# Paged key gathers of a decoding step: four issues at once, or one after each of four key transposes

## The reference, cut to what matters

```python
past_c = cache_ckv[l][page_table].reshape(n_s, past, KV_LORA)     # 8 x 4096 x 256
past_r = cache_krope[l][page_table].reshape(n_s, past, ROPE_DIM)  # 8 x 4096 x 32
...
q_lat = jnp.einsum('bthd,chd->bthc', q_nope, w_uk)
s = (jnp.einsum('bthc,blc->bhtl', q_lat, keys_c)
     + jnp.einsum('bthr,blr->bhtl', q_rope, keys_r)).astype(jnp.float32) * ATTN_SCALE
...
pr = jax.nn.softmax(s, axis=-1).astype(keys_c.dtype)
o_lat = jnp.einsum('bhtl,blc->bthc', pr, keys_c)
```

## Time and profile before

| | |
|---|---|
| median of 3 runs | 1775.27 us (1772.91 to 1775.78) |
| the profiled execution, its own time | 1764.69 us |
| its span, first to last instruction | 1762.9 us |
| TensorE busy in the span | 1696.1 us, 96% |
| VectorE, ScalarE, POOL busy | 536.5, 357.0, 163.1 us |
| mean granted TensorE clock | 0.98 of full speed |

### The profile page before, as it was taken

The page is one execution under the profiler, slowest core; times in us unless marked ns, Lnnn a source line. Parts: engine busy times, 40 slices in busy tenths (PEclk is TensorE's granted clock), DMA queues, the critical chain, the costliest instruction groups (busy, mean ns, idle before and its releaser), DMA issues.

```text
span 1762.9 us, 21779 instructions
## 1 busy us (share of the span) xinstructions
PE 1696.1 (96%) x9101; PEld 977.2 (55%) x9102; DVE 536.5 (30%) x1080; ACT 357.0 (20%) x690; POOL 163.1 (9%) x169
## 2 busy tenths in 40 slices
PE   7999999999999999999999999999999999999890
PEld 5556666666666666666666555554444444444340
DVE  1434242423422323232312454541112122221125
ACT  1122323223231121222121111101111111111115
POOL 1000000000001431111000000001111111111110
PEclk9999999999999999999999999989999999999995
DMA  7101111020114454332253442297999999999985
GB/s 209 50 24 40 49 36 49 25 79 30 61 49 138 162 187 172 132 132 108 70 198 108 155 158 84 94 376 279 390 369 387 383 396 385 388 388 392 382 298 201
DMA packets 103347, 335.47 MB, mean 190 GB/s; under 512 B 24346, under 2 KB 68450, under 8 KB 86868
## 3 DMA queue, kind: packets, MB, share of 16 engines
q1 hardware_dynamic: 88516, 274.11, 41.2%
q0 software_dynamic: 13568, 55.78, 9.9%
q10 hardware_dynamic: 1168, 4.23, 0.6%
HBM read 306.84 MB, written 34.45 MB: 194 GB/s over the span
## 4 chain that ended last, share of the span: by engine, by line
PE 90%; DMA 5%; DVE 2%; issue 1%; ACT 1%; POOL 0%; SPq 0%; DVEq 0%; POOLq 0%; ACTq 0%
PE psum L952 13%; PE psum L1062 9%; PE psum L1331 8%; PE psum L1336 7%; PE psum L1214 6%; PE psum L1228 5%; PE psum L1363 4%; PE psum L1357 4%; PE psum L989 4%; PE psum L877 3%; PE psum L1099 3%; PE psum L962 2%; DMA arena<-in_w_up 2%; PE psum L1007 2%; PE psum L1344 2%; PE psum L996 2%
## 5 line engine op out<-in xcount | busy, mean ns | idle before, releaser
L952 PE MATMUL psum<-arena 128*128 128x344 f32 x768 | 244.9, 456 | 0.0
L1062 PE MATMUL psum<-arena 128*128 128x344 f32 x576 | 182.3, 458 | 0.0
L952 PEld LDWEIGHTS psum<-arena 128*128 128x128 f32 x768 | 137.9, 190 | 63.8 <-issue 8.5
L1336 PE MATMUL psum<-arena 128*64 128x512 f32 x320 | 141.6, 595 | 0.7 <-ACT arena L1644 0.7
L1337 PE MATMUL psum<-arena 128*64 128x512 f32 x320 | 141.6, 595 | 0.0
L1331 PE MATMUL psum<-arena 128*128 128x512 f32 x320 | 139.8, 595 | 0.2 <-DVE arena L2213 0.2
L1062 PEld LDWEIGHTS psum<-arena 128*128 128x128 f32 x576 | 103.2, 190 | 53.0 <-issue 11.2
L1214 PE MATMUL psum<-arena 128*128 128x344 f32 x384 | 113.9, 460 | 1.1 <-ACT arena L1614 1.1
L1331 PEld LDWEIGHTS psum<-arena 128*128 128x128 f32 x320 | 60.0, 190 | 72.6 <-issue 72.1
L1228 PE MATMUL psum<-arena 128*128 128x512 f32 x224 | 99.2, 595 | 0.0
L1214 PEld LDWEIGHTS psum<-arena 128*128 128x128 f32 x384 | 74.3, 194 | 40.7 <-issue 3.7
(11 more groups left out here) (358 smaller groups left out, 2061.9 us busy)
## 6 DMA issues: line engine op xcount, KB each, us to landing
arena<-in_w_gate SPq DMA_DIRECT2D x32, 2048.0 KB, 20.3
arena<-in_w_up SPq DMA_DIRECT2D x32, 2048.0 KB, 25.9
arena<-in_w_down SPq DMA_DIRECT2D x32, 2048.0 KB, 32.1
arena<-in_w_in SPq DMA_DIRECT2D x33, 512.0 KB, 4.2
gates<-arena SPq DMA_DIRECT2D x16, 516.0 KB, 5.0
arena<-gates SPq DMA_DIRECT2D x16, 516.0 KB, 4.9
arena<-in_x_prompt SPq DMA_DIRECT2D x16, 512.0 KB, 4.2
arena<-in_w_o SPq DMA_DIRECT2D x1, 4096.0 KB, 18.3
```

Of the source, the lines that this page charges most:

```text
L952: ins = mm(out, wring[:, s, k, :], xT[:, k, b * SP3:(b + 1) * SP3], start=(k == 0), stop=(k == KD - 1))
L1062: ins = mm(psum[:, FB + t, 0:SP3], wring[:, u, k, :], xT[:, k, t * SP3:(t + 1) * SP3], start=(k == 0), stop=(k == KD - 1))
L1336: g = mm(psum[0:64, 2, :], xgT[:, xpar, k, 0:64], wg[:, k, :], start=(k == 0), stop=(k == KD - 1))
```

## The change

Each group but the first of every sample but the first now waits on POOL for a number of key steps of the sample before it: group 1 for `turn_keys(b - 1, 4)`, group 2 for `turn_keys(b - 1, 6)`, group 3 for `turn_keys(b - 1, 7)`. Group 0 is asked for as before.

```diff
             def load_cache(b):
                 for g in range(NLD):
+                    if b and g:
+                        pool.wait_ge(kt_done, NKG * (b - 1) + (5, 7, 8)[g - 1])
                     off = bass.IndirectOffsetOnAxis(ap=cache_idx[:, b * NLD + g:b * NLD + g + 1].bitcast(U32), axis=0)
                     pool.indirect_dma_start(kn[b % 2][:, g, :, :].rearrange("p r c -> p (r c)"), None, ckv_rows, off).then_inc(kn_ld[b % 2][g], 16)
                     pool.indirect_dma_start(kr_in[b % 2][:, g, :], None, kr_rows, off).then_inc(kn_ld[b % 2][g], 16)
```

## The result

The changed kernel takes 1763.28 us (median of 4 runs, 1762.93 to 1766.01) against 1775.25 us before (median of 4, 1772.91 to 1775.78): a ratio of 0.9937, interval 0.9922 to 0.9953. The prediction was 1775.3 us, range 1771.3 to 1779.0, with a chance of 0.85 for no difference. The time fell outside the range, on the side of rival B.

The account below looks back on a forecast made before the run. TensorE, busy for 1696.1 of 1762.9 us, was taken to set the pace; the terms summed as 0.0 + 0.0 + 0.0, leaving the median of before, 1775.3 us, range 1771.3 to 1779.0.

Parts of the forecast that it names:

- rival B: Sample attention: spreading the gather bursts helps, gain over 0.2%; at one microsecond a pass 7 us, 1768.3 us; chance 0.05.
- The margin of group 1: Gather of group 1 lands 7.3 us before `turn_rope(2, 0)` needs it, 4.7 with a landing of 9.1 us.
- the forecast of no difference: Whole kernel: time stays at 1775.3 us, a difference under 0.2%, 3.5 us, counting as the same; chance 0.85.
- the first term: TensorE beside the gather bursts: equal stretches of 20.61 us with and without one, so spreading gives back 7 x 0.00 = 0.0 us.
- The estimate of the slack: Behind `turn_keys(1, 4)`: 2.04 us free between the end of VectorE's key copy and the next key step.

Follow-up runs that it names:

- d3_groups_at_8: Against the change, groups 1, 2 and 3 all wait for the last key step of the sample before: 1780.55 us, 1.0035 of before.
- sets 1 and 4: Two occasions of timing kernels in turns with before on one chip: before 1763.94 and 1764.65 us, the change 0.9999 and 1.0002 of it.
- d1_before: The kernel before, unedited, timed against itself: 1773.21 us, 0.9990; its traced execution took 1768.90 us.
- set 2: An occasion of timing kernels in turns with before on one chip: before 1774.33 us, the change 1763.67 us, 0.9937.
- set 3: An occasion of timing kernels in turns with before on one chip, without the change itself: before 1783.64 us.
- void waits: Against the change, the 21 POOL waits are for key steps already done, so bursts stay: 1765.07 us, 1.0009 of before; on another occasion 1786.79 us, 1.0011.
- small rows: Against before, same eight issues, but latent gathers of samples 2 to 7 bring 1 KB a partition, not 8 KB: 1787.89 us, 1.0018.
- latents only: Against before, the rotary gathers of samples 2 to 7 are left out, four issues in a burst: 1764.98 us, 0.9998; again 1765.29 us, 1.0000.
- after landing: Each group of samples 1 to 7 is asked for when the one before it has landed: 1765.13 us, 1.0003 of before; again 1763.40 us, 0.9997.
- two and two: Against the change, groups 0 and 1 go at once, 2 and 3 together after the seventh key step: 1767.54 us, 0.9901 of before.

## Why the prediction was wrong

**What it had right.** The mechanics: four pairs behind their key steps, a pass of 36.52 us, no new wait, TensorE full. The margin of group 1 is real: asked for 10.5 us later it makes TensorE wait (`d3_groups_at_8`), by 1.9 us a pass. Latents asked for as in the change land after 5.7 us in the median, against 6.5 before. In sets 1 and 4 the forecast of no difference came true, 0.9999 and 1.0002.

**The step that failed** is the first term, "the burst costs TensorE 0.00 us a sample". For the profiled execution that is true. The error was to carry it to the runs. The text itself said that the profile lay 10.58 us below the median of the runs, more than three times the runs' own spread of 2.87, and then added it back as a constant. It was not a constant: it was some 11 us that the burst costs on a disturbed occasion, and the profile came from a quiet one. The same goes for rival B: it named what it needed (a slowness of VectorE's side caused by the bursts) and its price, one microsecond a pass, and got 0.05 because the profile showed none. `d1_before` has 7.2 us for seven bursts, just this price; the medians of the result and of set 2 differ by 12.0 and 10.7 us, and before in set 3 stands some 20 us above the change of the other sets.

**The estimate of the slack held** within some 0.2 us, and it is what turns lateness into time: behind `turn_keys(1, 4)`, 2.22 us late gives a wait of 0.30 us, and 4.51 us late one of 2.26, where 2.04 us of slack leave 0.18 and 2.47. The time goes up by more than the wait, 1.30 and 4.27 us a pass, in the second case in part by the granted clock. The prediction asked only whether an issue delays a copy while it runs, 0.95 us at most. It did not ask whether the signal between the engines could be late.

**What is shown and what is not.** Shown: the time lies in the sample attention; copies start up to 4.5 us after the key step that releases them, both engines at once and idle until then; this goes with the burst (gone without gathers, unchanged by void waits, unchanged by small rows, nearly gone with two groups at a time) and depends on where the burst falls. Shown for the change in two comparisons: 0.9937 both times. Not shown: what holds the signals back, and why only on some occasions. Sets 2 and 4 speak against the chip as the reason; what else was running near it at the time is not on record. Whether the number of issues in a burst or the number in flight decides was to be told by latents only and after landing, and both met quiet occasions only. A trace of before from the occasion of the result itself does not exist; that it had late copies is inferred from the equal ratio in set 2 and from the copies of 0.11 to 0.16 us in the profile after.

## What to carry to other kernels

Compare the profiled execution's own time with the median of the runs before reading anything else. If they differ by several times the runs' spread, the profile is of another course of the kernel or from another occasion, and "no wait here" holds for that one alone; look for what has little slack there. Compare two kernels on more than one occasion: in two of its four comparisons here the change looks worthless. And a burst of gathers from GpSimd's queue beside tightly coupled engines is a risk even when it costs nothing in the profile: spaced out, or sent two groups at a time, the same gathers cost nothing where the burst was harmless and were 0.6% (four steps) and 1% (two and two) faster where it was not.

## What the hardware showed that I had not expected

On some occasions signals from TensorE to ScalarE and VectorE were late by up to 4.5 us while eight indirect gathers went out in 9.7 us or just behind them, at 280 GB/s and at 99 GB/s alike (`e1_void_waits`, `e4_small_rows`). The Trainium skill, "SBUF — State Buffer", section "Who interferes with whom", says that DMA never contends with a compute engine. Of the instructions this agrees with the traces, since the late copies take their usual 0.59 and 0.69 us. It does not follow that gathers cost the other engines no time: here what came late was the signal between them. And the same kernel before had medians of 1764, 1774 and 1784 us on different occasions, while the change was at 1763.3 to 1764.9 in all four comparisons that it had.
